# The gates' row chain of a four-mixer layer, started later beside RWKV, on one NeuronCore

## The chip, the cores and the metric

One NeuronCore of a Trainium2 chip runs the whole program in one launch. The metric is the device time of one launch in microseconds (us), taken as the median of several runs. The kernel before took 2405.89 us (median of 3 runs, 2405.72 to 2407.83).

## The reference

The program computes a transformer layer for 256 tokens of width 2048 in fp32, and a second layer of attention branches behind it. The part that matters here is the first layer's projection and its mixers:

```python
n = rmsnorm(x, attn_norm[l])
u = n @ w_in[l]
u_gdn, u_mlstm, u_rglru, u_rwkv = jnp.split(u, MIXER_SPLITS, axis=-1)
...
# mlstm: per head and token
i_pre = i_raw.astype(jnp.float32) + b_i
log_f = jax.nn.log_sigmoid(f_raw.astype(jnp.float32) + b_f)
# gated deltanet: per head and token
beta = jax.nn.sigmoid(b_raw.astype(jnp.float32))
g = -jnp.exp(a_log) * jax.nn.softplus(a_raw.astype(jnp.float32) + dt_bias)
# rglru: a constant of its width
log_a = -RGLRU_C * r * jax.nn.softplus(-lam.astype(jnp.float32))
```

The four gate inputs (a_raw, b_raw, i_raw, f_raw) are 16 columns of u. Their sigmoid, softplus and running sums over the tokens are what this text calls the gates' chain. The second layer also projects a separate "memory" of 256 tokens, scaled and split into a high and a low part (the memory's split). RGLRU's constant is softplus(-lam).

## The kernel before, in words

Each fp32 weight tile is used as a high part and a low part. SyncE loads 1 MB units of weights into `raw` (3 buffers, two halves each). For each half ScalarE (ACT) casts `raw` to `ringH` (line 1378), VectorE (DVE) subtracts to get `ringL` (line 2005), and TensorE (PE) multiplies both with the activations (lines 693 and 694 in the RWKV blocks w0 to w6: 8 pairs of matmuls to a half). The rings hold 4 halves. Cast number h waits until TensorE has finished half h-4 (`use`); TensorE waits for `lo` of each half at its first matmul.

Every engine has its own instruction list, written by its own functions, and runs it strictly in that order. The order is made by `course`: one `Lane` per engine walks the same list of weight steps, and between the steps it takes the next piece of a side stage. A stage is a generator; a piece ends at a `yield`, which is called a halt. TensorE's stages lead, and the other engines put their pieces at the same steps. ACT's and DVE's casts and subtractions run up to three or four halves ahead of the step at which they stand in the list. So an engine's own place in its list may be reached later in time than TensorE reaches the same step.

`beside_rwkv` sets the order of the stages that lie beside the RWKV blocks: `scan` (the gates' chain, 14 halts), `mem` (the memory's split, 8 halts), `lambda` (RGLRU's constant), `mlstm`, `square`. It is advanced once for every 4 steps until block w3 is done, and once at each halt of the stage `rwkv` after that.

The pieces of `scan`, counted from 0, are these. Piece 1: sums of squares on TensorE. Pieces 2 and 3: the root and its reciprocal (ACT line 1532, DVE lines 2159 to 2169). Piece 4: ACT line 1537 (sigmoid), DVE line 2175. Piece 5: ACT lines 1540, 1542, 1544 (abs, exp). Piece 6: ACT line 1548 (log), DVE lines 2179, 2182, 2184 (softplus, and the running sum of the gates, ticked as "scan"). Piece 9: TensorE lines 762 and 763, which wait for "scan", and DVE lines 2190 to 2195. Piece 11: TensorE line 771, DVE lines 2200 to 2209. Piece 13: ACT line 1552.

The memory's split is ACT line 1498 and DVE line 2123, two tiles to each of its 8 pieces. The stage `rwkv` begins on DVE with constants (line 2365) and four token shifts (lines 2373 and 2376, one at each of its first four halts), each of which needs GpSimd's scaled rows (POOL line 2929), and these need DVE's drain of the block (line 2013). On TensorE its first matmul is line 928, at its fifth halt, then lines 938, 623, 896, 953 and 913. On ACT it begins with lines 1613 and 1615. The lines 1642 to 1650, 1606 and DVE lines 2354 and 2357 belong to it as well; line 913 waits for line 2357.

```python
for _ in L.stage("mem"):
    next(scan, None)
    yield
yield from scan
yield from L.stage("lambda")
```

Of the kernel before, what the change touches and what calls it, by code (L numbers as in the profile page):

```python
# [263 lines left out]
def beside_rwkv(L):  # L264
    scan = L.stage("scan")
    next(scan)
    yield
    for _ in L.stage("mem"):
        next(scan, None)
        yield  # L270
    yield from scan
    yield from L.stage("lambda")
    while not L.done("m0"):
        yield
    yield from L.stage("mlstm")
    yield from L.stage("square")


def course(L):
# [4 lines left out]
    L.run("turn")  # L284
    L.weave(L.stage("gates"), 2)
    side = beside_rwkv(L)
    while not L.done("w3"):
        next(side)
# [2948 lines left out]
```

## Time and profile before

| | |
|---|---|
| median of 3 runs | 2405.89 us |
| the profiled execution's own time | 2407.18 us |
| its span in the profile | 2405.4 us |
| instructions | 32321 |
| TensorE busy | 2385.3 us (99%) |
| VectorE busy | 1448.0 us (60%) |
| ScalarE busy | 1132.0 us (47%) |
| GpSimd busy | 97.2 us (4%) |
| DMA, mean over the span | 184 GB/s |

The span is counted from the first to the last recorded instruction, and the execution's own time is 1.8 us longer. A busy share is a mean over the whole program; at the place of the change DVE and ACT are far busier than their means. Matmuls overlap, so a start is a better measure of TensorE's progress than an end.

### The profile page before, as it was taken

To read this page: it belongs to the slowest core of one execution; us is meant where nothing else is said; L and a number is where in the kernel's file an instruction comes from. 1 tells how busy PE (TensorE), PEld (TensorE's weight loads), DVE (VectorE), ACT (ScalarE), POOL (GpSimd) and SP (SyncE) were. 2 spreads that over 40 slices of the span, in tenths; PEclk is the share of its full clock that TensorE was granted. 3 is DMA by queue.
4 is the path that set the end of the run, shared out by engine and by line. 5 is a ranking of instruction groups with operands and counts; after the bars stand their busy time and mean duration, and the time that the engine had idled before them with its cause. 6 is when DMAs were issued, how large, how long until landed. Compare 5 with 4: busy or idle time off the path is not lost.

```text
span 2405.4 us, 32321 instructions
## 1 busy us (share of the span) xinstructions
PE 2385.3 (99%) x13432; PEld 1986.3 (83%) x13432; DVE 1448.0 (60%) x1863; ACT 1132.0 (47%) x1429; POOL 97.2 (4%) x79
## 2 busy tenths in 40 slices
PE   8999999999999999999999999999999999999998
PEld 7787889888888888888888888888888888888887
DVE  7877657777755555555555665555555655555555
ACT  7635445553553444444444464445444455344444
POOL 1000011210000000000000140000000000000000
PEclk9999999999999999999999999999999999999999
DMA  9644355645655555555555566555545544655564
GB/s 304 197 130 125 122 158 197 203 162 201 201 181 190 190 192 184 185 191 193 189 183 189 179 242 209 187 168 171 174 149 196 182 148 150 201 190 192 191 238 140
DMA packets 245617, 443.55 MB, mean 184 GB/s; under 512 B 7392, under 2 KB 72544, under 8 KB 243168
## 3 DMA queue, kind: packets, MB, share of 16 engines
q1 hardware_dynamic: 241984, 423.65, 53.7%
q0 software_dynamic: 2912, 17.30, 1.9%
q8 instruction: 107, 1.75, 0.3%
q10 hardware_dynamic: 576, 0.53, 0.1%
q14 instruction: 38, 0.31, 0.0%
HBM read 430.97 MB, written 10.49 MB: 184 GB/s over the span
## 4 chain that ended last, share of the span: by engine, by line
PE 95%; DVE 2%; ACT 1%; issue 1%; DMA 0%; POOL 0%; SPq 0%; ACTq 0%; POOLq 0%; DVEq 0%
PE pp L664 25%; PE pp L666 24%; PE pp L665 24%; PE pp L693 8%; PE pp L694 4%; PE ps L623 2%; PE ps L1290 1%; PE ps L1304 1%; PE ps L812 1%; DVE ringL L2005 1%; DMA raw<-in_w_in 0%; PE ps L865 0%; PE pp L699 0%; PE pp L701 0%; PE pp L700 0%
## 5 line engine op out<-in xcount | busy, mean ns | idle before, releaser
L2005 DVE TENSOR_TENSOR ringL<-raw,ringH 128x1024 fp32r<-128x1024 f32 x779 | 962.6, 1242 | 687.0 <-ACT ringH L1378 684.1
L1378 ACT CAST ringH<-raw 128x1024 fp32r<-128x1024 f32 x779 | 814.2, 1049 | 977.7 <-PE pp L666 861.8
L664 PE MATMUL pp<-ringH,nS 128*128 128x512 f32 x1376 | 544.3, 396 | 0.0
L666 PE MATMUL pp<-ringH,nS 128*128 128x512 f32 x1376 | 536.7, 390 | 0.0
L665 PE MATMUL pp<-ringL,nS 128*128 128x512 f32 x1376 | 536.2, 390 | 0.0
L693 PE MATMUL pp<-nS,ringH 128*128 128x512 f32 x992 | 362.3, 407 | 7.0 <-DVE ringL L1999 3.2
L666 PEld LDWEIGHTS pp<-ringH,nS 128*128 128x128 f32 x1376 | 258.4, 188 | 54.4
L664 PEld LDWEIGHTS pp<-ringH,nS 128*128 128x128 f32 x1376 | 258.6, 188 | 52.3 <-issue 0.4
L665 PEld LDWEIGHTS pp<-ringL,nS 128*128 128x128 f32 x1376 | 258.7, 188 | 51.3 <-issue 0.2
L694 PE MATMUL pp<-nS,ringL 128*128 128x256 f32 x992 | 278.9, 281 | 0.0
L664 PE MATMUL pp<-ringH,xS 128*128 128x512 f32 x704 | 277.3, 394 | 0.0
L665 PE MATMUL pp<-ringL,xS 128*128 128x512 f32 x704 | 275.3, 391 | 0.0
L666 PE MATMUL pp<-ringH,xS 128*128 128x512 f32 x704 | 274.9, 390 | 0.0
L693 PEld LDWEIGHTS pp<-nS,ringH 128*128 128x128 f32 x992 | 187.2, 189 | 55.2 <-DVE ringL L2005 4.6
L694 PEld LDWEIGHTS pp<-nS,ringL 128*128 128x128 f32 x992 | 188.3, 190 | 0.1
L666 PEld LDWEIGHTS pp<-ringH,xS 128*128 128x128 f32 x704 | 132.2, 188 | 30.2
L664 PEld LDWEIGHTS pp<-ringH,xS 128*128 128x128 f32 x704 | 132.4, 188 | 28.3
L665 PEld LDWEIGHTS pp<-ringL,xS 128*128 128x128 f32 x704 | 132.4, 188 | 27.7
L664 PE MATMUL pp<-ringH,hS 128*128 128x512 f32 x352 | 140.0, 398 | 0.0
L665 PE MATMUL pp<-ringL,hS 128*128 128x512 f32 x352 | 139.0, 395 | 0.0
L666 PE MATMUL pp<-ringH,hS 128*128 128x512 f32 x352 | 138.9, 395 | 0.0
L2049 DVE TENSOR_TENSOR AR<-AR,pp 128x512 f32<-128x512 f32 x128 | 87.6, 686 | 37.1 <-PE pp L666 34.7
(405 smaller groups left out, 1942.9 us busy)
## 6 DMA issues: line engine op xcount, KB each, us to landing
raw<-in_w_in SPq DMA_DIRECT2D x189, 1024.0 KB, 5.1
raw<-in_ffn_w_gate SPq DMA_DIRECT2D x44, 1024.0 KB, 5.1
raw<-in_ffn_w_up SPq DMA_DIRECT2D x44, 1024.0 KB, 5.1
raw<-in_ffn_w_down SPq DMA_DIRECT2D x44, 1024.0 KB, 5.1
raw<-in_w_out SPq DMA_DIRECT2D x32, 1024.0 KB, 5.2
raw<-in_w_mem_kv SPq DMA_DIRECT2D x16, 1024.0 KB, 5.4
raw<-in_w_proj_a SPq DMA_DIRECT2D x8, 1024.0 KB, 5.1
raw<-in_w_proj_m SPq DMA_DIRECT2D x8, 1024.0 KB, 5.1
```

Source lines behind the costliest of these rows:

```text
L623: t = e.transpose(b[:, 128 * n:128 * n + 128], s, ident)
L664: mm(o, XH[:, ts(j)], WH, first, False)
L665: mm(o, XH[:, ts(j)], WL, False, False)
L666: t_of[0] = mm(o, XL[:, ts(j)], WH, False, last)
L693: mm(bk[j], WH[:, c], nS[:, k, :, :], first, False)
L694: t = mm(bk[j][:, T:2 * T], WL[:, c], XH, False, last)
L812: t = m1(o, lhs[c][:, n, :], rhs[c][:, n, :] if b is None else rhs[c][:, n, :, :], n == 0)
L1290: t = mm(b[:, ts(m - a)], qt, kt, m == a and r == 0, r == len(scores[m]) - 1)
L1304: t = mm(b[:, 0:values[m].shape[-1]], PT[:, ts(m)], values[m], m == 0, m == n - 1)
L1378: e.copy(ringH[:, h % NSPL, 0:nh * cols], raw[:, u % NRAW, h0 * cols:(h0 + nh) * cols]).then_inc(*hi.tick(h))
L2005: tt2(ringL[:, h % NSPL, o], raw[:, u % NRAW, h0 * cols:(h0 + nh) * cols], ringH[:, h % NSPL, o].bitcast(F32), SUB).then_inc(*lo.tick(h))
L2049: tt2(x, x, bk[b][:, :], ADD).then_inc(*drain_v.tick(*name))
```

## The change

The stage `scan` is no longer advanced at the last five halts of `mem`. After `mem`, it is advanced by two pieces at each halt, so its pieces 4 and 5 fall on the first halt of `rwkv`, 6 and 7 on the second, 8 and 9 on the third, 10 and 11 on the fourth, 12 and 13 on the fifth. Then five halts pass with nothing, and `lambda` follows. No operation is added to or taken from the source.

```diff
     scan = L.stage("scan")
     next(scan)
     yield
-    for _ in L.stage("mem"):
-        next(scan, None)
-        yield
-    yield from scan
+    for n, _ in enumerate(L.stage("mem")):
+        if n < 3:
+            next(scan)
+        yield
+    for _ in scan:
+        next(scan, None)
+        yield
+    for _ in range(5):
+        yield
     yield from L.stage("lambda")
```

Lines behind the edit carry numbers that are larger by 5 in the changed kernel (1378 is 1383 there, 762 is 767). The text below keeps the numbers of the kernel before, except in the rows of the changed order.

ACT, before, from the middle of the memory's split to its first RWKV instruction (`grow` holds the gates' rows, `memSt` the split memory; a bracket names what the instruction waits for):

```order
L1498 ACTIVATE memSt_51<-AR,prm 128x256
L1540 ACTIVATE grow<-grow 128x256 [waits s_gt_v]
L1542 ACT_TABLE_LOAD
L1542 ACTIVATE grow<-grow 128x256 [waits s_gt_a]
L1544 ACTIVATE small<-small 128x1 [waits s_h]
L1378 CAST ringH<-raw 128x1024 [waits s_use,s_raw2]
L1498 ACTIVATE memSt_51<-AR,prm 128x256 x2
L1548 ACT_TABLE_LOAD [waits s_gt_a]
L1548 ACTIVATE grow<-grow,csg 128x256 [waits s_c]
L1378 CAST ringH<-raw 128x1024 [waits s_use,s_raw2]
```

ACT, with the change, from the last cast ahead of the chain to its first RWKV instruction:

```order
L1383 CAST ringH<-raw 128x1024 [waits s_use,s_raw0]
L1542 ACT_TABLE_LOAD
L1542 ACTIVATE grow<-grow 128x256 [waits s_gt_v]
L1545 ACTIVATE grow<-grow 128x256 [waits s_gt_v]
L1547 ACT_TABLE_LOAD
L1547 ACTIVATE grow<-grow 128x256 [waits s_gt_a]
L1549 ACTIVATE small<-small 128x1 [waits s_h]
L1383 CAST ringH<-raw 128x1024 [waits s_use,s_raw1]
L1553 ACT_TABLE_LOAD [waits s_gt_a]
L1553 ACTIVATE grow<-grow,csg 128x256 [waits s_c]
L1383 CAST ringH<-raw 128x1024 [waits s_use,s_raw1]
L1618 ACT_TABLE_LOAD
```

The chain now stands behind the whole split, and one ring cast stands directly behind its piece 5.

DVE, with the change, from the first token shift of RWKV to the gates' running sum (before, L2175 stood two halves and L2184 one half ahead of the end of the split, far ahead of the shifts):

```order
L2378 TENSOR_TENSOR AR<-AR 128x512 [waits s_pool,s_mh2]
L2381 SCALAR_TENSOR_TENSOR AR<-AR,prm 128x256 [waits s_rw_v]
L2381 SCALAR_TENSOR_TENSOR AR<-AR,prm 128x256
L2180 TENSOR_SCALAR grow<-grow,small,csg 128x256 [waits s_gt_a,s_c,s_h]
L2010 TENSOR_TENSOR ringL<-raw,ringH 128x1024 [waits s_hi] x2
L2378 TENSOR_TENSOR AR<-AR 128x512 [waits s_pool]
L2381 SCALAR_TENSOR_TENSOR AR<-AR,prm 128x256 [waits s_rw_v]
L2381 SCALAR_TENSOR_TENSOR AR<-AR,prm 128x256
L2184 SCALAR_TENSOR_TENSOR grow<-grow 128x256 [waits s_gt_a]
L2187 TENSOR_SCALAR grow<-grow,small 128x256 [waits s_gt_v,s_gt_a]
L2189 SCALAR_TENSOR_TENSOR grow<-crst,grow 128x256 [waits s_gt_v]
```

The running sum (now L2189) stands behind two shifts of RWKV and two more subtractions of the ring.

TensorE, before, at the start of the third half behind the end of w3:

```order
L694 MATMUL pp<-nS,ringL 128x256
L771 MATMUL ps<-cm,grow 128x4 [waits s_gt_v]
L771 MATMUL ps<-cm,grow 128x4 x5
L693 MATMUL pp<-nS,ringH 128x512 [waits s_lo]
L694 MATMUL pp<-nS,ringL 128x256
```

TensorE, with the change, at the same place:

```order
L699 MATMUL pp<-nS,ringL 128x256
L767 MATMUL ps<-grow,cm 4x256 [waits s_gt_v]
L768 MATMUL ps<-grow,cm 4x256
L698 MATMUL pp<-nS,ringH 128x512 [waits s_lo]
L699 MATMUL pp<-nS,ringL 128x256
```

Lines 762 and 763 moved back by 20 pairs of matmuls to where line 771 was, and line 771 moved back by 10 pairs.

ACT also has one more table load: line 1642 now needs one of its own, because line 1582's (RGLRU's constant) has moved behind it. The pieces of `lambda` on ACT, DVE and POOL stand five halts later. SyncE's queue is the same.

## Rows read from the trace of the kernel before

**Rows 1.** The page: TensorE's busy time, and the chain that ended last.

```profile
PE 2385.3 (99%) x13432; PEld 1986.3 (83%) x13432; DVE 1448.0 (60%) x1863; ACT 1132.0 (47%) x1429; POOL 97.2 (4%) x79
...
PE 95%; DVE 2%; ACT 1%; issue 1%; DMA 0%; POOL 0%; SPq 0%; ACTq 0%; POOLq 0%; DVEq 0%
```

**Rows 2.** Waits of TensorE over the span: us in total, times, longest.

```profile
PE pp L693 <- DVE ringL L2005: 2.2, 4, 1.1
```

**Rows 3.** Timeline of PE: start, duration, line, tiles, idle before and its releaser.

```profile
46.22 0.40 PE L693 MATMUL pp<-nS,ringH 128*128 128x512 f32 x1
...
49.05 0.40 PE L693 MATMUL pp<-nS,ringH 128*128 128x512 f32 x1
...
57.68 0.51 PE L693 MATMUL pp<-nS,ringH 128*128 128x512 f32 x1
...
61.14 0.50 PE L693 MATMUL pp<-nS,ringH 128*128 128x512 f32 x1 [0.38 <-DVE ringL L2005]
...
65.24 0.47 PE L693 MATMUL pp<-nS,ringH 128*128 128x512 f32 x1 [1.05 <-DVE ringL L2005]
...
66.80 0.60 PE L762 MATMUL ps<-grow,cm 128*4 128x256 f32 x2
...
74.93 1.40 PE L771 MATMUL ps<-cm,grow 128*128 128x4 f32 x12
```

**Rows 4.** Timeline of DVE, 56 to 74 us.

```profile
56.09 0.40 DVE L2175 TENSOR_SCALAR grow<-grow,small,csg 128x256 f32<-128x256 f32 x1
56.41 1.21 DVE L2005 TENSOR_TENSOR ringL<-raw,ringH 128x1024 fp32r<-128x1024 f32 x1
...
59.88 1.21 DVE L2005 TENSOR_TENSOR ringL<-raw,ringH 128x1024 fp32r<-128x1024 f32 x1
...
62.37 0.43 DVE L2179 SCALAR_TENSOR_TENSOR grow<-grow 128x256 f32<-128x256 f32 x1 [0.49 <-ACT grow L1548]
...
63.29 0.69 DVE L2184 TENSOR_TENSOR_SCAN grow<-crst,grow 128x256 f32<-128x256 f32 x1
63.90 1.20 DVE L2005 TENSOR_TENSOR ringL<-raw,ringH 128x1024 fp32r<-128x1024 f32 x1
...
65.80 1.22 DVE L2005 TENSOR_TENSOR ringL<-raw,ringH 128x1024 fp32r<-128x1024 f32 x1
...
67.73 1.22 DVE L2005 TENSOR_TENSOR ringL<-raw,ringH 128x1024 fp32r<-128x1024 f32 x1
68.87 0.68 DVE L2013 TENSOR_TENSOR AR<-AR,pp 128x512 f32<-128x512 f32 x1
...
71.51 0.69 DVE L2373 TENSOR_TENSOR AR<-AR 128x512 f32<-128x512 f32 x1 [1.16 <-POOL AR L2929]
...
73.12 0.27 DVE L2190 MEMSET grow<- 128x256 f32 x1
```

**Rows 5.** Timeline of ACT, 56 to 70 us.

```profile
56.52 0.42 ACT L1540 ACTIVATE grow<-grow 128x256 f32<-128x256 f32 x1 [0.66 <-DVE grow L2175]
...
58.67 1.03 ACT L1378 CAST ringH<-raw 128x1024 fp32r<-128x1024 f32 x1
...
69.53 1.05 ACT L1378 CAST ringH<-raw 128x1024 fp32r<-128x1024 f32 x1 [2.29 <-PE pp L694]
```

**Rows 6.** Timeline of PE, 95 to 102 us.

```profile
95.01 0.63 PE L896 MATMUL ps<-cm,AR 128*64 128x2 f32 x16
...
101.42 1.10 PE L953 MATMUL ps<-AR,cm 128*128 128x512 f32 x2 [1.34 <-DVE small L2354]
```

**Rows 7.** Timeline of ACT, 96 to 101 us.

```profile
96.21 0.58 ACT L1418 COPY AR<-pp 128x512 f32<-128x512 f32 x1
...
99.80 1.28 ACT L1606 ACT_TABLE_LOAD   x1
```

**Rows 8.** Two stretches: length, busy time (count) of each engine, granted clock, DMA.

```profile
416.00:419.50 3.50, 3.50 (x19) 3.50 (x18) 1.83 (x4) 3.38 (x4) 0.00 (x0) 0.51 1.00 359
419.50:423.00 3.50, 3.50 (x31) 3.50 (x31) 3.03 (x4) 1.60 (x2) 0.53 (x1) 1.00 0.53 147
```

## The prediction

> **What bounds the kernel now.** I read the page first: TensorE is busy for 99% of the span and makes up 95% of the chain that ended last [rows 1]. So only what makes TensorE stand still, or run slower, can move the time. Next I read TensorE's waits: its waits for the low part of the ring are 2.2 us in the whole span, in four places [rows 2], and the timeline of PE puts two of them beside the memory's split, at 61.14 and 65.24 us [rows 3]. Then I read the timelines of DVE and ACT there, in the order of their lists, since what an engine does late is set by what stands ahead of it. All numbers below are starts in the profiled execution, which took 2407.18 us, 1.3 us over the median of 2405.89. Differences that I work out there I add to the median.
>
> I call the ring half whose first matmul is at 57.68 us A, and the next B (61.14), C (65.24), D, E, F, G. Without waits a half takes TensorE 2.83 us (46.22 to 49.05) [rows 3]. F begins where line 771 stands, at 74.93.
>
> **Part 1, the gates' chain leaves the memory's split: a gain of 1.5 us.** Line 2175 (56.09 to 56.41, so 0.32 us of DVE's time) no longer stands ahead of A's subtraction, which starts at 56.09 and ends at 57.30. TensorE can then start A at 57.53 instead of 57.68. From A's subtraction to B's DVE takes 59.88 - 56.41 = 3.47 us [rows 4], so B's starts at 59.56 and ends at 60.77. TensorE would be ready for B at 57.53 + 2.83 = 60.36, so it still waits 0.4 us and starts B at 60.82. A start after a wait costs it another 0.14 or so, so C comes at 63.8. C's subtraction now has only the split's two tiles ahead of it: subtraction and tiles take 65.80 - 63.90 = 1.90 us [rows 4], so it is done by 62.7 and C does not wait. F then begins at 63.8 + 3 x 2.83 = 72.3. Before, F began at 74.93, of which lines 762 and 763, that no longer stand ahead of it, were 74.93 - 65.24 - 8.49 = 1.2 us. So 74.93 - 1.2 - 72.3 = 1.45 us is saved.
>
> **Part 2, the chain's new place: a loss of 6.4 us.** TensorE reaches line 762 at the start of F, at 72.3, and must wait for line 2184. I follow what stands ahead of that line:
> - DVE: from B's subtraction at 59.56 come four subtractions (B to E) with three pairs of tiles between them: 3 x 1.90 + 1.14 (67.73 to 68.87) = 6.84, so line 2013 starts at 66.40 [rows 4].
> - From line 2013 to the end of RWKV's first shift is 73.12 - 68.87 = 4.25 us, in which DVE waits for GpSimd's line 2929 before line 2373 [rows 4]. GpSimd itself waits for line 2013, so this wait moves with it. Line 2175 starts at 70.65 and ends at 71.05.
> - ACT has loaded its table and done line 1537 by about 67 and then stands at line 1540 until 71.08. The cast of G is queued behind it. Before, that cast ran at 69.53, when TensorE freed its place [rows 5]; now it starts 58.67 - 56.52 = 2.15 us after line 1540 [rows 5], at 73.23, and ends at 74.28.
> - DVE's subtraction of G waits for that cast: 74.31, plus 1.14. Then the second shift, 73.12 - 71.51 = 1.61, then lines 2179 to 2184, 63.29 + 0.69 - 62.37 = 1.61 [rows 4]: 78.67. ACT's line 1548 (its load of 1.28 and 0.5 us of work behind G's cast) is through by 76, so it isn't the last.
>
> TensorE starts line 762 at 78.7 and has stood still for 6.4 us. DVE's list was already behind TensorE's before: it did the first shift at 71.51, when TensorE had passed the same step at 66.80. That was harmless because line 2184 stood ahead of the shifts (it ended at 63.98, 2.8 us before line 762). Behind line 762 nothing else is late: line 771 comes ten pairs, 3.5 us, later, at about 83.3, and line 2195 is due at about 82.1 by the same steps; the ring is two halves ahead.
>
> **Part 3, RGLRU's constant later: a gain of 0.7 us.** TensorE waits 1.34 us at line 953 [rows 6], because two activations and a table load for the constant stand ahead of a cast on ACT, and DVE's chain stands behind that. With them gone line 953 starts on time, at 101.42 - 1.34 = 100.08. But line 1642 has its own table load now, and a load takes 1.28 us [rows 7]. From ACT's line 1418 to the load of line 1606 was 99.80 - 96.21 = 3.59 [rows 7]; with 1.28 more, and line 1418 starting when TensorE ends its block at 95.06, that load ends at 101.2, and line 2357, for which line 913 waits, at about 101.7. Line 913 could start when the two matmuls of line 953 are through, about 1.0 us behind its start, at 101.1. So 0.6 us of the 1.34 is given back as a wait there, all against the times before. The constant's small DVE operations now lie beside RWKV's inversion, where DVE in turn waits for TensorE: I cost them at nothing, and if that slack is used up they would add their 0.2 us each to a step of it. The memsets on GpSimd cost nothing, since they have no reader near.
>
> The Trainium skill prices such a table switch higher (ScalarE: Activation LUTs, What ACT_TABLE_LOAD costs): about 2.66 us, with a drain behind the 1.28 us of the load. By it the sum would grow by 1.4 us for line 1542's load on the chain of part 2 and by 2.1 us at line 913, that is to +9.2. The trace has room for less: the 2.15 us from line 1540 to the cast [rows 5] hold line 1542's load of 1.28 and three activations, and 0.87 us is left for those, so no drain of that size. I take 1.28.
>
> **Part 4, the clock: a loss of 1.4 us.** The trace before has no idle time of TensorE near 6 us, so this is a bound. One stretch in the middle of the span shows the price of 1.2 GHz: it ran so from 416.0 to 419.5 us, after a stretch with many matmuls of one column: 19 matmuls there against 31 in the same time after it [rows 8], so 3.5 x 12/31 = 1.4 us lost. The lower end for our case is 0 (no fall, or one that is over when TensorE starts again; a gain has no cause). The upper end is 2.8, two such stretches. I take one, 1.4, since an idle engine is at least as inactive as one with single columns. The Trainium skill says the same of idleness (TensorE: Matmul & The Clock Gate, Why this matters for your kernels): gaps in TensorE's work bring it to the lower clock, and it needs steady work to return.
>
> **Sum**: -1.45 + 6.4 - 0.7 + 1.4 = +5.65 us, 2411.5 us. About 0.2% (4.8 us) is what a measurement here can tell from no change, so this is slower by slightly more than that.
>
> **The rivals.**
> - *The clock does not fall or is back at once.* The sum is +4.25, 2410.1 us. For it: no row shows a fall from idleness alone. The wait would be there, and the time within 0.2%.
> - *DVE is in time.* If the running sum were done before 72.3 there would be no wait at line 762, and the change gives -1.45 - 0.7 = -2.2, 2403.7 us, not slower. That is decided at line 2184's end: it must come 6.4 us sooner than I find. Against it stand three hard orders (the POOL wait, ACT's stop at line 1540, the cast of G). For it: I may have an operation at the wrong step.
> - *More is lost behind it.* The clock stays low for two stretches (+1.4), and line 913 gives back all 1.34: +7.7, 2413.6 us. For it: DVE's line 2195 is through only 1.2 us before line 771 needs it, so a late piece can make it wait as well.
> - *Table loads carry a drain.* +9.2 from the pieces above, 2415.1 us. By the page's rule, above; the trace is against it.
> - *The change does nothing*: the time stays at 2405.9. The order lists show the pieces moved, so this is hardly possible.
>
> **How the numbers follow.** Forecast 0.46, clock unharmed 0.24, DVE in time 0.10, more lost 0.15, drain 0.03, nothing 0.02. Each sum is uncertain by about 1 us. Slower by over 0.2%: most of the forecast (0.36), a quarter of the case with the clock unharmed (0.06), all of more lost and drain (0.18): 0.60. Faster by over 0.2% would take 4.8 us, more than all waits that the change can remove (1.45 + 1.34 and 0.4 for B): 0.02. Within: 0.38. The range leaves out DVE in time, nothing and the drain (0.15 together): 2406.0 is below the clock unharmed with a part of the wait missing, 2415.0 above more lost with its uncertainty. The forecast's own range is 2410 to 2413.
>
> **What would show it.** In the profile after: TensorE idle for about 6.4 us before line 762, released by DVE's line 2184, at 72 to 79 us; no idle time before C, under 0.6 before B; ACT idle for about 4 us before line 1540; G's cast at about 73 us; no wait at line 953 and a short one at line 913; a clock below 1 right behind line 762; one more ACT_TABLE_LOAD. If TensorE's wait before line 762 is under 3 us, part 2 is wrong. If it is there and the time is within 2 us of before, part 3 or the stretches behind it gave back what I don't see.

## The result and the profile after

The changed kernel took 2412.51 us (median of 12 runs, 2411.92 to 2412.98), the kernel before 2406.90 us in the same comparison (12 runs, 2405.72 to 2407.83). The ratio is 1.0025, with a 95% interval of 1.0017 to 1.0032. So the change made the kernel 5.6 us slower, where 5.65 was forecast. The time itself is 1.0 us above the forecast of 2411.5, because the kernel before came out 1.0 us higher than in the three runs from which the forecast counts. The profiled execution of the changed kernel has a span of 2410.4 us against 2405.4, 5.0 more.

All lines in rows of the changed kernel carry numbers larger by 5. The text keeps the old numbers. First, the waits of TensorE over the whole span (us in total, times, longest), which answer to [rows 2]:

```profile
PE ps L767 <- DVE grow L2189: 7.4, 1, 7.4
PE pp L698 <- DVE ringL L2004: 3.3, 2, 1.7
PE ps L918 <- DVE small L2362: 1.6, 3, 0.8
PE ps L738 <- POOL grow L2951: 1.2, 1, 1.2
PE pp L698 <- DVE ringL L2010: 1.1, 3, 0.4
```

There is a new first entry: line 762 (now 767) waits 7.4 us for the gates' running sum, line 2184 (now 2189). The waits for the ring (now L2010) have gone from 2.2 to 1.1 us, and the wait of line 953 is no longer in the list.

The timeline of PE at the places of [rows 3] and [rows 6]:

```profile
57.34 0.40 PE L698 MATMUL pp<-nS,ringH 128*128 128x512 f32 x1
...
61.00 0.51 PE L698 MATMUL pp<-nS,ringH 128*128 128x512 f32 x1 [0.32 <-DVE ringL L2010]
...
72.06 0.40 PE L698 MATMUL pp<-nS,ringH 128*128 128x512 f32 x1
...
79.95 1.02 PE L767 MATMUL ps<-grow,cm 128*4 128x256 f32 x2 [7.38 <-DVE grow L2189]
...
86.27 1.40 PE L776 MATMUL ps<-cm,grow 128*128 128x4 f32 x12
...
107.87 1.10 PE L958 MATMUL ps<-AR,cm 128*128 128x512 f32 x2
109.22 1.09 PE L918 MATMUL ps<-cm,small 128*64 128x128 f32 x16 [0.25 <-DVE small L2362]
```

Half B still waits 0.32 us, C not at all. By the modelled end of the matmul ahead of it, TensorE came to line 762 at 79.95 - 7.38 = 72.57. By starts it is 0.16 us sooner: the last ring matmul ahead of it started at 72.06, and such starts are 0.35 us apart, so the next was due at 72.41. Line 953 (958) starts without a wait, and line 913 (918) waits 0.25.

The timeline of DVE, which answers to [rows 4]:

```profile
65.52 1.21 DVE L2010 TENSOR_TENSOR ringL<-raw,ringH 128x1024 fp32r<-128x1024 f32 x1
66.65 0.67 DVE L2018 TENSOR_TENSOR AR<-AR,pp 128x512 f32<-128x512 f32 x1
...
70.47 0.69 DVE L2378 TENSOR_TENSOR AR<-AR 128x512 f32<-128x512 f32 x1 [2.33 <-DMA mem_hold<-memSt]
71.19 0.88 DVE L2381 SCALAR_TENSOR_TENSOR AR<-AR,prm 128x256 f32<-128x256 f32 x2
71.99 0.41 DVE L2180 TENSOR_SCALAR grow<-grow,small,csg 128x256 f32<-128x256 f32 x1
72.31 1.22 DVE L2010 TENSOR_TENSOR ringL<-raw,ringH 128x1024 fp32r<-128x1024 f32 x1
75.64 1.23 DVE L2010 TENSOR_TENSOR ringL<-raw,ringH 128x1024 fp32r<-128x1024 f32 x1 [2.10 <-ACT ringH L1383]
...
79.21 0.69 DVE L2189 TENSOR_TENSOR_SCAN grow<-crst,grow 128x256 f32<-128x256 f32 x1
```

The chain to the running sum is visible with its releasers. DVE stands before its first shift, here until a DMA has stored the memory's third tile (it was GpSimd in [rows 4]), and then for a cast on ACT. The timeline of ACT, which answers to [rows 5]:

```profile
66.98 0.42 ACT L1542 ACTIVATE grow<-grow 128x256 f32<-128x256 f32 x1
72.43 0.42 ACT L1545 ACTIVATE grow<-grow 128x256 f32<-128x256 f32 x1 [5.04 <-DVE grow L2180]
72.87 1.28 ACT L1547 ACT_TABLE_LOAD   x1
74.16 0.42 ACT L1547 ACTIVATE grow<-grow 128x256 f32<-128x256 f32 x1
...
74.58 1.03 ACT L1383 CAST ringH<-raw 128x1024 fp32r<-128x1024 f32 x1
```

ACT stood for 5.0 us at line 1540 (1545), and the cast queued behind it ran at 74.58. The granted clock, in stretches of the changed kernel (length, busy time and count of PE, PEld, DVE, ACT, POOL, PE clock, DMA share, GB/s):

```profile
77.00:80.00 3.00, 0.05 (x1) 0.05 (x2) 2.82 (x7) 2.97 (x4) 0.00 (x0) 0.50 0.37 130
80.00:83.80 3.80, 3.80 (x10) 2.06 (x11) 3.73 (x8) 2.73 (x4) 0.00 (x0) 0.50 0.41 109
83.80:88.00 4.20, 4.20 (x31) 3.87 (x30) 2.42 (x4) 1.53 (x2) 0.84 (x1) 1.00 0.43 151
299.00:302.50 3.50, 3.50 (x33) 3.11 (x31) 1.87 (x6) 1.88 (x3) 0.00 (x0) 1.00 0.02 5
```

The clock fell to 1.2 GHz while TensorE stood idle and was still there when it started again, up to 83.8 us. The last row is read beside one of the kernel before, at the same instructions:

```profile
293.20:296.60 3.40, 3.40 (x13) 2.91 (x12) 1.67 (x4) 0.48 (x2) 0.00 (x0) 0.51 0.06 7
```

There the kernel before ran at 1.2 GHz for 3.4 us and the changed one did not.

### The profile page after: what moved, and what is told of

Same layout as the page of the kernel before. It is cut to its first block, busy times and chain, and to the rows that moved or that the text cites. A ratio compares the mean times of both kernels' runs of the same rounds, so it can differ in the third digit from the quotient of the medians.

```text
span 2410.4 us, 32321 instructions
## 1 busy us (share of the span) xinstructions
PE 2386.8 (99%) x13432; PEld 1986.8 (82%) x13432; DVE 1446.4 (60%) x1863; ACT 1133.7 (47%) x1430; POOL 100.3 (4%) x79
## 4 chain that ended last, share of the span: by engine, by line
PE 96%; DVE 2%; ACT 1%; DMA 1%; issue 0%; ACTq 0%; DVEq 0%
PE pp L669 25%; PE pp L671 24%; PE pp L670 24%; PE pp L698 9%; PE pp L699 4%; PE ps L628 2%; PE ps L1295 1%; PE ps L1309 1%; PE ps L817 1%; DVE ringL L2010 0%; PE ps L870 0%; DMA mem_hold<-memSt 0%; PE pp L704 0%; PE pp L706 0%; PE pp L705 0%
## 5 line engine op out<-in xcount | busy, mean ns | idle before, releaser
L2010 DVE TENSOR_TENSOR ringL<-raw,ringH 128x1024 fp32r<-128x1024 f32 x779 | 961.5, 1240 | 691.0 <-ACT ringH L1383 688.1
```

What stands on the lines that cost most here:

```text
L2010: tt2(ringL[:, h % NSPL, o], raw[:, u % NRAW, h0 * cols:(h0 + nh) * cols], ringH[:, h % NSPL, o].bitcast(F32), SUB).then_inc(*lo.tick(h))
```

## The experiments

Every kernel was timed in 5 rounds beside the kernel before on the same chip. The first four share one set of runs of before (2406.39 us), the next four another (2406.02 us), the last two a third (2406.17 us). Labels of pieces and halves are those of the prediction. The first six are edits of `beside_rwkv` alone. In the variants of the changed kernel the loop behind `mem` takes this form, where the tuple says how many pieces fall on each halt and `wait` is the number of empty halts before `lambda`:

```diff
-    for _ in scan:
-        next(scan, None)
-        yield
-    for _ in range(5):
-        yield
+    for pieces in COUNTS:
+        for _ in range(pieces):
+            next(scan)
+        yield
+    next(scan, None)
+    for _ in range(WAIT):
+        yield
     yield from L.stage("lambda")
```

The added lines shift the numbers of the rows below by 7 against the kernel before, where not said otherwise.

**One piece at a halt**: COUNTS of ten ones, WAIT 0.

> The changed kernel with the chain's pieces 4 to 13 taken one at a halt instead of two; RGLRU's constant starts at the same halt as in the changed kernel. Theory (TensorE reaches line 762 before DVE's running sum is done, because both stand too close): line 762 now comes five halts behind piece 4 and line 2184 two halts behind it, so the wait before line 762 (7.4 us) is gone, the gain beside the memory's split (1.3 us) and the one at lines 953 and 913 stay: 2404.5 us, against 2406.9 before. Rival (the loss is DVE's and ACT's load, moved beside RWKV's shifts, whatever the halts): the same work lies there, TensorE's idle time between 65 and 110 us stays near 7 us and the time over 2410.

Measured: 2405.02 us, ratio 0.9996 (0.9987 to 1.0005). The timeline of PE has these three waits between 40 and 118 us:

```profile
60.89 0.50 PE L700 MATMUL pp<-nS,ringH 128*128 128x512 f32 x1 [0.32 <-DVE ringL L2012]
...
73.80 0.50 PE L700 MATMUL pp<-nS,ringH 128*128 128x512 f32 x1 [1.55 <-DVE ringL L2012]
...
100.14 0.67 PE L960 MATMUL ps<-AR,cm 128*128 128x512 f32 x1 [1.15 <-DVE small L2361]
```

The wait before line 762 is gone. The timeline of DVE, then that of PE, show the running sum and line 762:

```profile
80.65 0.69 DVE L2191 TENSOR_TENSOR_SCAN grow<-crst,grow 128x256 f32<-128x256 f32 x1
```

```profile
88.60 0.59 PE L769 MATMUL ps<-grow,cm 128*4 128x256 f32 x2
```

The running sum, now behind three shifts, came even 1.4 us later than in the changed kernel, but line 762 came 7 us behind its end. So the place of line 762, and not DVE's load, made the wait. Two smaller waits were uncovered: at F (1.55 us) and at line 953 (1.15 us), since lines 2190 to 2195 now stand in DVE's list ahead of line 953's operand. The rival fails in its 7 us, but the three waits together, 3.0 us, are no less than the 2.8 us of the kernel before.

**RGLRU's constant alone**, on the kernel before (numbers here are larger by 2):

```diff
     yield from scan
+    for _ in range(5):
+        yield
     yield from L.stage("lambda")
```

> The kernel before, with RGLRU's constant five halts later, and nothing else. Theory: line 953's wait of 1.34 us goes and 0.3 to 0.6 us of it comes back at line 913 behind the new table load, so 2406.0 us, 0.7 to 1.0 under before. Rival 1 (the new table load eats it all): 2406.9, with a wait of 1.3 us at line 913. Rival 2 (the wait at 953 vanished in the changed kernel only because TensorE was late there): the wait at line 953 stays at about 1.3 us, time 2406.9.

Measured: 2404.47 us, ratio 0.9991 (0.9983 to 1.0000). In the timeline of PE the two waits at B and C stand as before, and of the two at lines 953 and 913 one small one is left:

```profile
61.72 0.51 PE L695 MATMUL pp<-nS,ringH 128*128 128x512 f32 x1 [0.38 <-DVE ringL L2007]
...
65.82 0.47 PE L695 MATMUL pp<-nS,ringH 128*128 128x512 f32 x1 [1.01 <-DVE ringL L2007]
...
101.97 1.09 PE L915 MATMUL ps<-cm,small 128*64 128x128 f32 x16 [0.25 <-DVE small L2359]
```

So the wait at line 953 goes without TensorE being late, and both rivals fall. The trace gives a gain of 1.0 us. The median says 1.9, but the interval reaches to nothing.

**The constant at its old halt, in the changed kernel**: COUNTS (2, 2, 2, 2, 2), WAIT 0.

> The changed kernel without the five empty halts before RGLRU's constant, which so starts at the same halt as in the kernel before. Theory: the wait before line 762 is as in the changed kernel (7.4 us); DVE had no slack left at line 953 in the changed kernel, so ACT's 1.7 us of the constant come back there as a wait of about 1.3 us: 2413.5. Rival (after a wait of 7.4 us on TensorE, DVE and ACT are far enough ahead at line 953): no wait there and 2412.5, so that moving the constant was worth nothing in this pair.

Measured: 2413.08 us, ratio 1.0032 (1.0019 to 1.0044). The timeline of PE:

```profile
80.95 1.01 PE L769 MATMUL ps<-grow,cm 128*4 128x256 f32 x2 [8.32 <-DVE grow L2191]
...
110.62 1.10 PE L960 MATMUL ps<-AR,cm 128*128 128x512 f32 x2 [1.31 <-DVE small L2361]
```

The wait of 1.31 us at line 953 is back, as the theory had it. By these waits the move of the constant is worth about 1 us with either order of the chain. The wait at line 762 was 0.9 us longer than in the changed kernel, though nothing ahead of it differs: DVE's first shift began 1.0 us later (71.46), when the store of the memory's tile had landed. This profiled execution took 2415.00 us, 1.9 over the median of 5 runs, so it is a long one.

**The ring cast ahead of piece 5**: COUNTS (1, 3, 2, 2, 2), WAIT 5.

> The changed kernel with the chain's pieces taken 1, 3, 2, 2, 2 at the five halts: piece 5 (lines 1540 to 1544 on ACT) moves behind the ring cast that it held up. Lines 762 and 2184 stand at the same halts. Theory (the cast queued behind ACT's wait at line 1540 is one link of the chain): the cast runs at about 69.6 us instead of 74.6, DVE does not wait 2.1 us for it, and line 2184 ends about 1.9 us sooner: wait before line 762 5.5 us, 2410.6 us if the clock does the same. Rival (the link is not in the chain, DVE's own work is): the wait stays at 7.4 us and the time at 2412.5.

Measured: 2410.74 us, ratio 1.0017 (1.0009 to 1.0026). The timeline of ACT, then that of PE:

```profile
67.77 1.05 ACT L1385 CAST ringH<-raw 128x1024 fp32r<-128x1024 f32 x1 [0.18 <-DMA raw<-in_w_in]
73.21 0.42 ACT L1547 ACTIVATE grow<-grow 128x256 f32<-128x256 f32 x1 [4.38 <-DVE grow L2182]
```

```profile
79.03 1.02 PE L769 MATMUL ps<-grow,cm 128*4 128x256 f32 x2 [6.26 <-DVE grow L2191]
```

The cast ran at 67.8 instead of 74.6, and the wait fell by 1.1 us, not by 1.9, though the time is the expected one. Here DVE's first shift began at 71.24, 0.8 us later than in the changed kernel, on the store of the memory's tile. From that shift to the start of line 2184 were 78.28 - 71.24 = 7.04 us against 79.21 - 70.47 = 8.74, so the cast was a link worth 1.7 us. The rival falls.

**Line 762 one halt later**: COUNTS (2, 2, 1, 2, 2, 1), WAIT 4.

> The changed kernel with pieces 2, 2, 1, 2, 2, 1 at its halts: line 762 on TensorE stands one halt (ten pairs of matmuls, 3.5 us) later, pieces 4 to 7 and RGLRU's constant where they were. Theory (the wait is the distance between TensorE's arrival and line 2184's end, which does not move): wait 7.4 - 3.5 = 3.9 us, 2409.0 us if TensorE's clock still falls and about 2407.2 if it does not. Rival (the late thing is not line 2184 but DVE as a whole, and what moves later meets another late piece): wait still over 6 us, 2412.

Measured: 2408.93 us, ratio 1.0012 (1.0003 to 1.0021). The timeline of PE:

```profile
74.48 0.50 PE L700 MATMUL pp<-nS,ringH 128*128 128x512 f32 x1 [1.66 <-DVE ringL L2012]
...
77.90 0.47 PE L700 MATMUL pp<-nS,ringH 128*128 128x512 f32 x1 [0.38 <-DVE ringL L2012]
80.85 1.01 PE L769 MATMUL ps<-grow,cm 128*4 128x256 f32 x2 [2.01 <-DVE grow L2191]
```

The three waits together are 4.05 us where 3.9 were expected, but half of that stands in front of the ring halves F and G. In the changed kernel these waits were hidden behind the one at line 762. From the end of the last wait on the clock was at 1.2 GHz again (0.51 from 80.7 to 84.1 us). The rival's figures fail, but what it says of DVE as a whole is in part so: the ring's low halves are late as well.

**Line 762 two halts later**: COUNTS (2, 2, 1, 0, 2, 2, 1), WAIT 3.

> The same with pieces 2, 2, 1, 0, 2, 2, 1: line 762 two halts later (7.0 us). Theory: wait before it at most 0.4 us and no fall of the clock from it; but TensorE now goes straight into F, whose subtraction ends at 73.5 us because DVE stood for the memory tile's DMA before its first shift, so a wait of 1.0 to 1.6 us appears there: 2405.0 us. Rival: as above, 2409 or more.

Measured: 2405.41 us, ratio 0.9998 (0.9989 to 1.0006). The timeline of PE:

```profile
74.02 0.50 PE L700 MATMUL pp<-nS,ringH 128*128 128x512 f32 x1 [2.08 <-DVE ringL L2012]
...
77.45 0.47 PE L700 MATMUL pp<-nS,ringH 128*128 128x512 f32 x1 [0.34 <-DVE ringL L2012]
...
81.51 0.50 PE L700 MATMUL pp<-nS,ringH 128*128 128x512 f32 x1 [1.05 <-DVE ringL L2012]
```

No wait is left at line 762. The ring is late in three places instead, 3.5 us together. In this profile the granted clock was full from 15 us to near the end, so no fall came from it. Each against the kernel before of its own comparison, the times with zero, one and two halts are 5.6 and 2.9 us over and 0.6 us under. The first halt took 3.3 us from the waits (7.4 to 4.05), almost its own 3.5. The second took only 0.6 us (4.05 to 3.5), and the fall of the clock: what is left is the lateness of the ring's low halves.

**The memory's second and third tile exchanged**, in the changed kernel (numbers larger by 5):

```diff
-enumerate((0, MU + 988, SC, SC + 2048))]
+enumerate((0, SC, MU + 988, SC + 2048))]
...
-                    if n == 4:
+                    if n == 2:
                         e.wait_ge(*nx_v.at("lo", 15))
...
-                e.wait_ge(s_mh[2], 16)
+                e.wait_ge(s_mh[1], 16)
```

> The changed kernel with the places of the memory's second and third staged tile exchanged, so that DVE's first shift needs the store of the second tile (landed by about 65 us), not of the third (landed at 70.4 us). Theory (the store's landing is the last link before line 2373 in the changed kernel, by 1.1 us over GpSimd): line 2373 starts at 69.3 instead of 70.5, wait before line 762 6.3 us, 2411.4. Rival (the store is a mere coincidence and GpSimd's line 2929 sets it): unchanged, 2412.5.

Measured: 2410.40 us, ratio 1.0018 (1.0009 to 1.0026). The timeline of DVE, then that of PE:

```profile
69.86 0.69 DVE L2378 TENSOR_TENSOR AR<-AR 128x512 f32<-128x512 f32 x1 [1.16 <-POOL AR L2934]
```

```profile
79.35 1.01 PE L767 MATMUL ps<-grow,cm 128*4 128x256 f32 x2 [6.42 <-DVE grow L2189]
```

DVE's first shift now waits for GpSimd, 1.16 us, as in [rows 4], and the wait at line 762 is 1.0 us shorter. The rival falls: the store was the last link.

**All of it together**: the exchange, and COUNTS (1, 1, 2, 1, 1, 1, 1, 1, 1), WAIT 1.

> The exchange of tiles, and pieces 1, 1, 2, 1, 1, 1, 1, 1, 1 at the halts: piece 9 (line 762, lines 2190 to 2195) at the fifth halt, ahead of RWKV's chain to line 953 and behind the running sum by over one halt; RGLRU's constant where it is in the changed kernel. Theory: no wait at line 762, none or under 0.5 us at F, none at line 953, 0.3 at line 913: 1.3 us from the memory's split and 0.8 from lines 953 and 913 under before, 2404.0 or slightly less. Rival (each place only hands its wait to the next): 2405 to 2406.4, with new waits of 1 us or more between 72 and 110 us.

Measured: 2403.01 us, ratio 0.9989 (0.9980 to 0.9998). Between 44 and 110 us, waits of TensorE are this one entry:

```profile
PE pp L700 <- DVE ringL L2012: 0.3, 1, 0.3
```

It is faster than both kernels: 3.0 us under the one before. It was then timed beside the kernel with the constant alone moved.

> The fastest kernel so far, once more and beside the next one on the same chip, 5 rounds each. Theory (the gains of the memory's split, 1.3 us, and of RGLRU's constant, 0.8 us, add up): 2403.0, 1.3 us under the kernel with the constant alone moved.

> The kernel before with RGLRU's constant alone moved, once more beside the last one. Theory: 2404.3, 1.3 us over it; its waits at B and C (0.38 and 1.01 us) are still there. Rival (the fastest kernel is faster only by the chance of the clock or of the chip): within 0.5 us of the last one.

Measured: 2403.11 us, ratio 0.9987 (0.9979 to 0.9996), and 2403.30 us, ratio 0.9988 (0.9979 to 0.9997). By the medians the rival holds: 0.2 us lie between the two. The profiled executions suggest why a gain of 1.3 us in waits need not show. In the first one TensorE ran at 1.2 GHz for 3.4 us:

```profile
411.70:415.10 3.40, 3.40 (x18) 3.40 (x18) 1.73 (x4) 3.37 (x5) 0.00 (x0) 0.51 0.97 361
```

In the second the clock was full throughout, from 17 us to near the end:

```profile
17.00:400.00 383.00, 377.71 (x3518) 315.56 (x3517) 277.66 (x481) 205.68 (x294) 35.89 (x28) 1.00 0.52 167
400.00:2390.00 1990.00, 1989.96 (x9861) 1656.18 (x9861) 1158.32 (x1360) 913.51 (x1113) 59.21 (x43) 1.00 0.57 187
```

The lowest of 11 runs was 2401.64 and 2401.78 us for the combined kernel, and 2402.89 both times for the other, 1.1 to 1.3 us apart. That agrees with the waits removed, but it is not a test. Whether the memory's split free of the chain is worth its 1.3 us in the median stays open.

The traces allow a sharper comparison than the medians. From the last ring matmul ahead of A to the first one behind line 913, TensorE does the same 264 matmuls in every kernel. The timeline of PE, two rows from the kernel before and then one from the changed kernel:

```profile
57.17 0.40 PE L693 MATMUL pp<-nS,ringH 128*128 128x512 f32 x1
...
103.47 0.51 PE L693 MATMUL pp<-nS,ringH 128*128 128x512 f32 x1
```

```profile
110.24 0.50 PE L698 MATMUL pp<-nS,ringH 128*128 128x512 f32 x1
```

Before, the stretch took 103.47 - 57.17 = 46.30 us; in the changed kernel 110.24 - 57.34 = 52.90. The differences, beside those of the medians, each against its own runs of before:

| kernel | this stretch, us | median, us |
|---|---|---|
| changed | +6.6 | +5.6 |
| one piece at a halt | 0.0 | -1.4 |
| constant alone, twice | -1.0, -1.0 | -1.9, -2.9 |
| constant at its old halt | +9.0 | +6.7 |
| cast ahead of piece 5 | +5.9 | +4.4 |
| line 762 one halt later | +3.5 | +2.9 |
| line 762 two halts later | +1.2 | -0.6 |
| tiles exchanged | +5.4 | +4.4 |
| all of it together, twice | -1.5, -2.5 | -3.0, -3.1 |

The order of the kernels is nearly the same in both columns, but every median lies 0.5 to 2.3 us lower than its stretch. A gain of 1 or 2 us in a median is therefore not all a gain of the edit.

## Why the prediction was right

The step that decided it, part 2, held. It said that line 762 waits for line 2184, that DVE's first shift, ACT's stop at line 1540 and the cast of G are its links, and that line 771 is not late. One piece at a halt and the first halt show the wait to be the distance between the two lines, the cast experiment shows ACT's link, and the exchange shows the link before the first shift.

Point by point, with what the trace of the changed kernel gives:

- *Part 1, -1.45 us.* F was due at 72.41. Without line 762 it was reached at 74.93 - 1.2 = 73.7 before, so -1.3. The profile of after was already 0.17 us behind at the matmul ahead of A (57.34 against 57.17), so the change itself is worth -1.5, as forecast. The residue at B was 0.32 where 0.4 was forecast, and C did not wait.
- *Part 2, +6.4 us.* From 72.41 to 79.95 it was +7.5, of which the profile counts 7.4 as idle. The step that was short is "from line 2013 to the end of RWKV's first shift": I let DVE wait there for GpSimd alone, by the row of before. In the changed kernel GpSimd was done at 69.2 us, but the store of the memory's third tile, issued at 61.77, took 8.7 us to land, until 70.5. Line 2373 starts 3.82 us after line 2013 instead of 2.64. Line 2373 waits for the store in both kernels. Before, the store (61.91, and 9.4 us) landed at 71.3 and GpSimd was done at 69.63 + 1.78 = 71.41, so the store was hidden behind GpSimd by 0.1 us only. GpSimd's work moved up with line 2013, the store did not, and I did not ask for it.
- *Part 3, -0.7 us.* It was -1.0: 1.34 gone at line 953, and line 913 starts 1.35 us behind line 953 instead of 1.02.
- *Part 4, +1.4 us.* Line 771 came 86.27 - 79.95 = 6.3 us after line 762. Ten pairs less, the 8.1 us of [rows 3] make 4.6, so the low clock cost 1.7.
- *Not in the sum*: the stretch at 293 us, which was at 1.2 GHz in the profile of before and not in the one after, 1.8 us. TensorE's lag against the kernel before is 6.8 us up to there and 5.0 behind it. It explains the 5.0 of this pair of profiles. None of the other ten profiles has this stretch at 1.2 GHz either, only that of the kernel before. If the kernel before has it in many executions and the others in few, that is why all medians in the table above lie below their stretches; this is not shown.

So -1.5 + 7.5 - 1.0 + 1.7 = +6.7 at 110 us, where the count of the stretch gives 6.6, and 5.0 at the end. The medians are 5.6 apart. That the forecast of 5.65 met this within 0.1 us is luck: beside the change it was 1.0 us short, most of it the missed store, and something behind 110 us, in the main the clock's stretch at 293 us as far as the profiles show, took about as much back. The mechanism was right, the figure partly by chance.

The Trainium skill (ScalarE: Activation LUTs, What ACT_TABLE_LOAD costs) gives 2.66 us for a table switch, a drain included. The trace does not bear that out: in the changed kernel line 1542's load began at 72.87 and its activation at 74.16, 1.29 us later, and ACT's cast follows line 1540 by 74.58 - 72.43 = 2.15 us, as before. The Trainium skill (TensorE: Matmul & The Clock Gate, Why this matters for your kernels) has gaps in TensorE's work lower its clock. Here the trace agrees: the clock was at 0.50 from 77.0 us, in the idle time before line 762.

## What to carry to other kernels

Where engines run fixed lists beside each other, a piece that one engine produces and another waits for must keep its distance in time, not in steps: an engine whose list is filled with look-ahead work can reach the same step several microseconds after the waiting one. Moving such a piece back relieves the place it leaves, but everything in front of it, and everything queued behind its own waits, becomes part of its latency. Before costing the new chain, list every wait of each instruction in it, those that never showed in the trace too, since an old delay may have hidden them.

## What the runs showed of the hardware

TensorE's clock fell in the changed kernel in an idle time of 7.4 us and cost 1.7 us after it. It also fell after much less. In the kernel with line 762 one halt later it fell 0.3 us before line 762, at the end of the wait of 2.0 us (the granted clock was 1.00 from 78.9 to 80.5 us and 0.50 from 80.6 to 84.0). In the combined kernel it fell with no wait at all, while TensorE was working, after two groups of matmuls with 2 and 4 columns:

```profile
95.00:98.40 3.40, 3.40 (x13) 2.92 (x12) 3.33 (x7) 3.37 (x6) 1.24 (x1) 0.51 0.00 0
```

A second profile of that kernel has 1.00 in the same stretch, with 22 matmuls instead of 13. The same instructions, in the same order, fall or do not. What such a stretch costs can be read between two profiles: 1.0 us here (-1.5 against -2.5 in the table), 1.5 us between the two profiles of the kernel with the constant alone moved, where one has a stretch at 414 us and the other has not, 1.8 us at 293 us. It is the likeliest part of the spread of 1 to 3.7 us that runs of one kernel show, but that is not shown, and nothing here shows what decides the fall.

Executions also differ before they reach the edit. The last ring matmul ahead of A started between 56.90 and 57.76 us in the twelve profiles, and differed by 0.2 and 0.3 us between two profiles of the same kernel. So times of single instructions in two profiles are best compared from a common start.

The store of 1 MB of the memory's split, which SyncE issues among the loads of weights, decided a start on DVE. In four kernels whose lists differ only behind that point (the changed one, line 762 two halts and one halt later, the constant at its old halt) it took 8.7, 9.5, 9.1 and 9.6 us to land, and DVE's first shift began at 70.5, 70.9, 71.4 and 71.5 us.
